# Experts phase: down products one pair late, down weights asked one expert late, rows gathered before the first weights

## The reference, cut to what matters

```
def run_block(args):
    xblk, e = args
    return (jax.nn.silu(xblk @ w_gate[e]) * (xblk @ w_up[e])) @ w_down[e]
```

## Time and profile before

| | |
|---|---|
| median of three runs | 4578.34 us |
| the profiled execution | 4582.33 us |
| its span | 4580.5 us |
| mean granted TensorE clock over the span | 0.912 of full speed |
| PE busy, share of the span | 3719.3 us, 81% |
| experts phase of layer 0, first weights asked to last down product | 1945.1 to 2647.4 us |
| experts phase of layer 1, the same | 3808.1 to 4502.6 us |

### The profile page before, as it was taken

The page is one execution under the profiler, slowest core; times in us unless marked ns, Lnnn a source line. Parts: engine busy times, 40 slices in busy tenths (PEclk is TensorE's granted clock), DMA queues, the critical chain, the costliest instruction groups (busy, mean ns, idle before and its releaser), DMA issues. The chain is left out here.

```text
span 4580.5 us, 88111 instructions
## 1 busy us (share of the span) xinstructions
PE 3719.3 (81%) x34274; PEld 2393.4 (52%) x34275; DVE 1880.4 (41%) x4412; ACT 1370.2 (30%) x3094; POOL 590.2 (13%) x926
## 2 busy tenths in 40 slices
PE   4998995698898866589999817998999766999972
PEld 1786553588888845133333306895666552333321
DVE  3322554677777554300000055415777651000004
ACT  2211564366665322011111112114666411111111
POOL 0000000144444130200000021100000011000001
PEclk6999997899999987699999958999999877999986
DMA  7221001222222154786899962213000414679995
GB/s 291 89 89 70 9 10 41 43 65 80 74 76 75 37 174 174 228 340 262 304 363 388 397 253 102 89 58 145 10 10 10 133 73 198 242 299 387 408 428 210
DMA packets 252931, 771.21 MB, mean 168 GB/s; under 512 B 77908, under 2 KB 166248, under 8 KB 221896
## 3 DMA queue, kind: packets, MB, share of 16 engines
q1 hardware_dynamic: 200488, 639.85, 37.5%
q10 hardware_dynamic: 37584, 78.13, 4.5%
q0 software_dynamic: 14544, 48.79, 2.8%
HBM read 641.22 MB, written 117.60 MB: 166 GB/s over the span
## 5 line engine op out<-in xcount | busy, mean ns | idle before, releaser
L3238 PE MATMUL ex_bY<-ex_w,ex_aT 128*64 x880 | 389.1, 595 | 73.7 <-DVE ex_aT L3301 73.7
L3238 PE MATMUL ex_bG<-ex_w,ex_xT 128*64 x880 | 405.2, 615 | 39.4 <-SPq L3159 26.7
L3241 PE MATMUL ex_bG<-ex_w,ex_xT 128*64 128x512 f32 x880 | 405.3, 615 | 0.0
L3241 PE MATMUL ex_bY<-ex_w,ex_aT 128*64 128x512 f32 x880 | 389.4, 595 | 0.0
L3241 PE MATMUL ex_bU<-ex_w,ex_xT 128*64 128x512 f32 x880 | 386.6, 592 | 0.0
L3238 PE MATMUL ex_bU<-ex_w,ex_xT 128*64 x880 | 386.6, 592 | 0.0
L3299 DVE TENSOR_TENSOR ex_a<-ex_sg,ex_bU 128x512 f32<-128x512 f32 x55 | 37.9, 688 | 813.6 <-PE ex_bU L3241 813.6
L3238 PEld LDWEIGHTS ex_bG<-ex_w,ex_xT 128*64 128x64 f32 x880 | 123.9, 142 | 302.6 <-issue 302.6
L3238 PEld LDWEIGHTS ex_bY<-ex_w,ex_aT 128*64 128x64 f32 x880 | 116.0, 137 | 299.9 <-issue 299.9
L1036 DVE TENSOR_SCALAR_CACHE_REDUCE ad_p<-ad_S 128x512 f32<-128x512 f32 (+1 forms) x384 | 215.6, 600 | 99.8 <-PE ad_S L946 99.7
L3238 PEld LDWEIGHTS ex_bU<-ex_w,ex_xT 128*64 128x64 f32 x880 | 120.6, 137 | 247.4 <-issue 247.4
(11 more groups left out here) (467 smaller groups left out, 8545.5 us busy)
## 6 DMA issues: line engine op xcount, KB each, us to landing
ex_w<-in_moe_w_gate SPq DMA_DIRECT2D x64, 2048.0 KB, 12.2
ex_w<-in_moe_w_up SPq DMA_DIRECT2D x64, 2048.0 KB, 16.4
ex_w<-in_moe_w_down SPq DMA_DIRECT2D x64, 2048.0 KB, 15.0
yb_dram<-ex_y ACTq DMA_DIRECT2D x55, 512.0 KB
rt_mw<-in_mod_w SPq DMA_DIRECT2D x24, 1024.0 KB, 9.4
n_mw<-in_mod_w SPq DMA_DIRECT2D x16, 1024.0 KB, 8.8
kb_dram<-rs_pout SPq DMA_DIRECT2D x60, 256.0 KB, 2.8
rs_KB<-kb_dram SPq DMA_DIRECT2D x120, 128.0 KB, 2.7
```

The lines of the kernel that those rows point to most:

```text
L3238: nc.tensor.matmul(bank[0:BR, :], stationary[:, k, 0:BR], w[:, ds(slot0 + (offset + k * n), 512)], start=k == 0, stop=k == tiles - 1)
L3241: m = nc.tensor.matmul(bank[BR:P, :], stationary[:, k, BR:P], w[:, at:at + 512], start=k == 0, stop=k == tiles - 1)
```

## The change

On PE a pair's down products move behind the next pair's gate and up products and row transposes; its transposes of `a` come after the down products of the pair before. The first pair's gate, up and transposes stand ahead of the loop, the last pair's down products behind it. Each of the three parts of a pair now reads and splits its own code from the table (`where`). The first gate products wait for the first half of the turned rows only, and for the second half at k = 4. On SyncE the down weights of expert o - 1 are asked in the step of expert o, behind its gate and up; each ask reads expert and pair count anew; nothing is asked before GpSimd has issued the first gather (`first_asked`). On GpSimd the gather comes first and the clearing after it. ScalarE and VectorE follow PE's order. The number of matmuls, transposes, copies and bytes is as before.

```diff
@@ -3158,31 +3158,45 @@
-    def step(o, u, free, before):
+    def ask(part, o, u, free):
         e = load(sp, ds(o + T_EXP, 1), NE - 1)
-        tiles = load(sp, ds(o + (T_PEND - WR), 1), NPM, 1) if free else None
-        for part in range(3):
-            fetch(u, e, tiles, part)
-            if before is not None:
-                arrived(*before, part)
-
+        fetch(u, e, load(sp, ds(o + (T_PEND - WR), 1), NPM, 1) if free else None, part)
+
+    def step(o, u, free_gu, free_down, times, seen):
+
+        v = (u - 1) % WR
+        for part in range(2):
+            ask(part, o, u, free_gu)
+            if times is not None:
+                arrived(v, times, part)
+        if times is not None:
+            ask(2, o - 1, v, free_down)
+            if seen is not None:
+                arrived((u - 2) % WR, seen, 2)
+
+    sp.wait_ge(first_asked, 1)
     for o in range(WR):
-        step(o, o, False, (o - 1, 1) if o else None)
+        step(o, o, False, False, 1 if o else None, 1 if o > 1 else None)
...
-    with sp.Fori(1, NE // WR) as i:
+    step(WR, 0, True, False, 1, 1)
+
+    rounds = (NE - WR - 1) // WR
+    with sp.Fori(1, rounds + 1) as i:
         for u in range(WR):
-            step(WR * i + u, u, True, (u - 1, i + 1) if u else (WR - 1, i))
-    left = NE % WR
-    for u in range(left):
-        step(NE - left + u, u, True, (u - 1, NE // WR + 1) if u else (WR - 1, NE // WR))
-    for part in range(3):
+            step(WR * i + 1 + u, (1 + u) % WR, True, True, i + 1, i + 1 if u else i)
+    for o in range(WR * (rounds + 1) + 1, NE):
+        step(o, o % WR, True, True, (o - 1) // WR + 1, (o - 2) // WR + 1)
+    for part in range(2):
         arrived((NE - 1) % WR, (NE - 1) // WR + 1, part)
+    ask(2, NE - 1, (NE - 1) % WR, True)
+    for o in range(NE - 2, NE):
+        arrived(o % WR, o // WR + 1, 2)
...
@@ -3192,11 +3206,12 @@
 def _(pool):
-    nc.gpsimd.memset(zero[:, :], 0.0).then_inc(zeroed, 1)
-    n = load(pool, slice(T_NP, T_NP + 1), NPM)
     nc.gpsimd.tensor_copy(idx[:, :], tok[:, 0:1]).then_inc(idx_done, 1)
     pool.wait_ge(idx_done, 1)
     nc.gpsimd.indirect_dma_start(x[:, :], None, rows[:, :], bass.IndirectOffsetOnAxis(idx[:, 0:1], 0)).then_inc(x_in, 16)
+    pool.sem_inc(first_asked, 1)
+    nc.gpsimd.memset(zero[:, :], 0.0).then_inc(zeroed, 1)
+    n = load(pool, slice(T_NP, T_NP + 1), NPM, 2)
     with pool.Fori(0, n) as i:
...
@@ -3223,46 +3238,66 @@
-    turn(0, False)
-    with pe.Fori(0, n) as i:
-
+    def where(i):
         code = load(pe, ds(i + T_CODE, 1), WR * WR * (NE + 1) - 1, WR * WR)
-        need, slot1 = code // (WR * WR), code % WR
-        slot0 = (code % (WR * WR)) // WR * WCOLS
-
-        def products(bank, stationary, tiles, offset, n, done):
-
-            for u in range(WR):
-                with pe.If(slot1 == u):
-                    for k in range(tiles):
...
-        pe.wait_ge(w_ready[0], need)
-        pe.wait_ge(xT_done, 2 * i + 2)
-        products(bG, xT, KT, 0, EH, g_done)
-        pe.wait_ge(w_ready[1], need)
-        products(bU, xT, KT, UP, EH, u_done)
-        turn(i + 1, True)
-
-        pe.wait_ge(a_done, i + 2)
+        return code // (WR * WR), (code % (WR * WR)) // WR * WCOLS, code % WR
+
+    def products(bank, stationary, at, tiles, offset, n, done, second=None):
+
+        need, slot0, slot1 = at
+        for u in range(WR):
+            with pe.If(slot1 == u):
+                for k in range(tiles):
+                    if second is not None and k == tiles // 2:
+                        pe.wait_ge(xT_done, second)
+                    nc.tensor.matmul(bank[0:BR, :], stationary[:, k, 0:BR], w[:, ds(slot0 + (offset + k * n), 512)],
...
+                    col = u * WCOLS + offset + k * n
...
+                m.then_inc(done, 1)
+
+    def hidden(i, part):
+        at = where(i)
+        pe.wait_ge(w_ready[part], at[0])
+        if part == 0:
+            pe.wait_ge(xT_done, 2 * i + 1)
+            products(bG, xT, at, KT, 0, EH, g_done, 2 * i + 2)
+        else:
+            products(bU, xT, at, KT, UP, EH, u_done)
+
+    def turn_hidden(i):
+
+        pe.wait_ge(a_done, i + 1)
         for k in range(HT):
             t = nc.tensor.transpose(bA[:, k * P:(k + 1) * P], a[:, k:EH:HT], ident[:, :])
         t.then_inc(atr, 1)
+
+    def down(i):
+        at = where(i)
         pe.wait_ge(aT_done, i + 1)
         pe.wait_ge(ye_act, i + 1)
         pe.wait_ge(ye_dve, i + 1)
-        pe.wait_ge(w_ready[2], need)
+        pe.wait_ge(w_ready[2], at[0])
         for b in range(2):
-            products(bY[b], aT, HT, DOWN + b * 512, D, y_done)
+            products(bY[b], aT, at, HT, DOWN + b * 512, D, y_done)
+
+    turn(0, False)
+    hidden(0, 0)
+    hidden(0, 1)
+    turn(1, True)
+    turn_hidden(0)
+    with pe.Fori(1, n) as i:
+        hidden(i, 0)
+        hidden(i, 1)
+        turn(i + 1, True)
+        down(i - 1)
+        turn_hidden(i)
+    down(n - 1)
...
-    turned(0)
-    with act.Fori(0, n) as i:
+    def gated(i):
         act.wait_ge(g_done, i + 1)
-
-        act.wait_ge(a_done, i + 1)
         nc.scalar.activation(sg[:, :], bG[:, :], ACT.Silu).then_inc(sg_done, 1)
-        turned(i + 1)
-        act.wait_ge(y_done, 2 * i + 1)
+    def copied(i, least=None):
+        act.wait_ge(y_done, 2 * i + 1 if least is None else least)
...
+    turned(0)
+    gated(0)
+    turned(1)
+    with act.Fori(1, n) as i:
+
+        act.wait_ge(a_done, i)
+        gated(i)
+        turned(i + 1)
+        copied(i - 1)
+    copied(n - 1, 2 * n)
...
-    dve.sem_inc(a_done, 1)
-    with dve.Fori(0, n) as i:
+    def multiplied(i):
...
+    def turned(i):
...
+    def copied(i):
         dve.wait_ge(y_done, 2 * i + 2)
...
+    multiplied(0)
+    turned(0)
+    with dve.Fori(1, n) as i:
+        multiplied(i)
+        copied(i - 1)
+        turned(i)
+    copied(n - 1)
```

More of the change, by code:

```diff
@@ L3134, in experts_phase @@
             "g_done", "u_done", "sg_done", "a_done", "atr", "aT_done", "y_done", "ye_act", "ye_dve", "y_out"))
-        go, ended, filled, zeroed = (s.sem(n) for n in ("go", "ended", "filled", "zeroed"))
+        go, ended, filled, zeroed, first_asked = (s.sem(n) for n in ("go", "ended", "filled", "zeroed", "first_asked"))
         zero = s.sb("zero", [P, D])
@@ L3212, in _ @@
                 pe.wait_ge(c_in, 16)
-                n = load(pe, slice(T_NP, T_NP + 1), NPM)
+                n = load(pe, slice(T_NP, T_NP + 1), NPM, 2)
                 def turn(i, again):
@@ new lines, in where @@
+                    return code // (WR * WR), (code % (WR * WR)) // WR * WCOLS, code % WR
[7 more added lines that the diff above has]
+                                nc.tensor.matmul(bank[0:BR, :], stationary[:, k, 0:BR], w[:, ds(slot0 + (offset + k * n), 512)],
+                                                 start=k == 0, stop=k == tiles - 1)
+                                col = u * WCOLS + offset + k * n
+                                m = nc.tensor.matmul(bank[BR:P, :], stationary[:, k, BR:P], w[:, col:col + 512], start=k == 0, stop=k == tiles - 1)
+                            m.then_inc(done, 1)
@@ L3292, in _ @@
             def _(dve):
-                n = load(dve, slice(T_NP, T_NP + 1), NPM)
+                n = load(dve, slice(T_NP, T_NP + 1), NPM, 2)
                 dve.sem_inc(ye_dve, 1)
-                dve.sem_inc(a_done, 1)
-                with dve.Fori(0, n) as i:
+                def multiplied(i):
                     dve.wait_ge(sg_done, i + 1)
```

9 lines of the change are left out of this document (2 added, 7 removed).

## The result

| | before | after |
|---|---|---|
| median of the runs | 4578.45 us (4574.96 to 4579.10, 4 runs) | 4608.19 us (4602.55 to 4613.15, 4 runs) |
| the profiled execution, its span | 4582.33, 4580.5 us | 4602.55, 4600.8 us |
| mean granted TensorE clock | 0.912 | 0.906 |

The medians are 29.7 us apart; the ratio of the runs is 1.0058, 95% interval 1.0045 to 1.007, or 27 us. The changed kernel is slower. The prediction said 4571 us, range 4544 to 4594.

The account below looks back on a forecast made before the run. PE was taken to bound each layer's earlier pairs and DMA the last ones. Layer 1's +4.1 and layer 0's -11.9 gave -7.8 us on the median 4578.3, forecast 4571 us, range 4544 to 4594.

Parts of the forecast that it names:

- the start: Start of each layer: gather issued 0.9 us earlier, half the turned rows suffice; -2.0 us in layer 0, -1.7 in layer 1.
- first pair and last pair: Ends of each layer's phase: +6.3 us said for layer 0, -1.1 for layer 1.
- the pairs between, without the circle: Pairs where PE sets the pace: overlap hides the wait before down products; -32.2 us in layer 0, -22.9 in layer 1.
- the circle: Last pairs: loads wait for late down products and PE for loads; 39.2 us per pair against 31.2; +16.0 and +31.9.
- The wait before the last down products of layer 0: Layer 0's end: last down weights asked only when the previous pair's down products end; +7.5 us.
- My link of 14.1 us: In the circle: gate weights asked 1.93 us after the down ask, landing 12.2 us after that, 14.1 together.
- A pair without weight waits: Gate to gate on PE in the first regime: 22.3 us after the change, bounds 22.1 and 22.4.
- The rival that would have put it down to PE's queue: Table read and branches before down products not hidden: 0.5 us a pair, +22, 4593 us; chance 0.18.
- First stretch: First 24 pairs of layer 0 and 20 of layer 1, DMA allowance included: -33.4 and -24 us.
- the prediction's own test: For the whole sum: the forecast falls if either of the two large terms, -57 and +53, is off by a third.
- My allowance for DMA: First stretch: 6.5 us in layer 0 and 5 in layer 1 added for DMA work exceeding PE's time.
- the wait only moves: Wait leaves the down products for another place, pair stays near 23.8 us: +66, 4637 us; chance 0.03.

Follow-up runs that it names:

- tail_old_6: Changed kernel with the last six pairs of each layer in the old order on PE, ScalarE and VectorE; 4559.11 us against 4587.07 before, ratio 0.9939.
- turns_split: Changed kernel with the four transposes of `a` put two and two behind each half of the down products; ratio to before 1.0111.
- pe_one_read: Changed kernel with one table read on PE for gate and up products instead of two; ratio to before 1.0052, pair 22.67 us.
- signal_early: Changed kernel with SyncE waiting for and signalling an expert's gate weights ahead of the down ask; ratio to before 1.0021.
- rows_first: Kernel before, with only the gather issued ahead of the clearing and the first weights asked behind it; 4577.14 us against 4587.07, ratio 0.9978.
- tail_3_and_6_early: Changed kernel with the old order for the last three pairs of layer 0 and six of layer 1, plus early gate signal; 4547.65 us against 4589.41, 0.9904.

## Why the prediction was wrong, point by point

Said and measured, in us against before, each counted from the phase's own first transfer; measured from the two traces:

| step | layer 0, said | measured | layer 1, said | measured |
|---|---|---|---|---|
| the start | -2.0 | -7.1 | -1.7 | -5.0 |
| first pair and last pair | +6.3 | +8.9 | -1.1 | -0.4 |
| the pairs between, without the circle | -32.2 | -13.5 | -22.9 | -8.6 |
| the pair before the circle (layer 1) | | | 0 | +0.9 |
| the circle | +16.0 | +16.7 | +31.9 | +30.0 |
| the pair behind it | | | -2.1 | -1.1 |
| sum | -11.9 | +5.0 | +4.1 | +15.8 |

- **The circle: right**, in place, mechanism and size. 38.7 us on the mean of four pairs against 39.2; DMA's share 0.85 and 0.82 against "about 0.8"; gate products wait 14 to 15 us, as said. The first of the four takes 36.94 us and not 38 to 40: its gate products still run at the full clock, 6.91 us against 8.3 to 9.6. One name was wrong: the ask ahead of the gate of b is that of expert a - 1, not of a. It waits for the same pair, p - 2, so the time is the same. The wait before the last down products of layer 0 is there too: 8.91 us at 2642.71, on the timeline of PE,
```profile
2642.71 1.11 PE L3253 MATMUL ex_bY<-ex_w,ex_aT 128*64 x1 [8.91 <-SPq L3159]
```
 and `tail_old_6` confirms it by taking it away. My link of 14.1 us was right in sum, but not as I read it: with the asks 0.7 us apart it was 13.7.
- **A pair without weight waits: the second step that failed, a term mis-sized**, 22.3 said, 22.67 measured, outside my bounds of 22.1 to 22.4. I took "about 0.1 at each change of kind" once for the pair. The rows above give it: 6.92 + 6.97 + 7.02 for the products instead of 20.7, 1.09 and 0.68 for the transposes instead of 1.1 and 0.5. `turns_split` shows 0.17 us for each further change. Before, the two groups of transposes stood side by side, and a pair had two changes of kind; after, they stand apart, and it has four. Two more at 0.17 make 0.35. Over 24 and 19 pairs it is 0.37 x 43 = 16 us. The rival that would have put it down to PE's queue named nearly the right time, 22.8, for the wrong reason: see `pe_one_read`.
- **First stretch: the step that failed.** I allowed 6.5 and 5 us for DMA (the figures beside them give 5.4 and 4.2), nothing for SyncE and nothing for the clock. Measured were 560.4 - 24 x 22.67 = 16.3 us in layer 0, and 442.9 - 19 x 22.67 = 12.2 in layer 1, 17 more than allowed: 20.5 us are waits for a late signal, 8.0 us the lower clock in the pairs behind them. I had followed the *asks* behind the new wait, but not the *signals*: `arrived` stands in the same queue, so it is late too, wherever three experts come in two pairs. I had the rule in hand, what is queued behind the waiting instruction, and applied it to the last pairs alone. `signal_early` takes all of it away but the wait of pair 24. Of the -55.1 us said for the pairs between, -22.1 came; by the prediction's own test, a large term off by a third, the forecast as a whole falls. My allowance for DMA was not baseless: with the signals in time the loads take back a part behind the stretch.
- **The start: mis-sized the other way.** I let the gather's 11.7 us stand; ahead of the weights it takes 8.1. The two starts together gave -12.1 us instead of -3.7, and `rows_first` alone is 9.9 us faster than before. The half of the turned rows gave the 0.7 said: from turn to gate 2.35 us and not 3.10.
- **Net.** The first stretch lost 33 us (16 + 17) against the forecast, the start gave 8 back, the rest lost 4: 28.6 us between the -7.8 said and the +20.8 of the two phases. More than half of it, 17 us, is one thing: what stands behind a waiting down ask, which I saw in the last pairs and missed in the first stretch. That the forecast did not miss by more is luck, for the start erred the other way. The chance of 0.03 for the rival "the wait only moves" was too small: of the 63 us of idle time that left the down products, 20 came back before gate products of the first stretch, and the clock took 8 more.
- **The bandwidth.** After and `tail_3_and_6_early` have stretches at 405 to 425 GB/s and a share of 1.00; the DMA engines are full there, at a rate well over 358. The 358 GB/s that the Trainium skill gives in "DMA: Bandwidth & Descriptors", section "Where 436 GB/s comes from", is no bound for this kernel. Another page of the Trainium skill, "Perfetto Trace Analysis", section "Roofline", says why: the figure is the share when both cores of a pair draw, and a single core is bound by its DMA engines at about 435 GB/s. By that one, the traces agree: no stretch shown here goes over 425 GB/s.

## What to carry to other kernels

Where a change puts a wait into an in-order queue, list everything that stands behind it in that queue, signals as much as asks, at every place of the loop and not only where the resource is scarce. A row that says "waits for SyncE" does not say that data is late: compare the landing with the product before the wait is priced. A pair that is longer without idle time wants a look at the granted clock and at the pair before it. Work moved behind later work frees its buffers later; where the ring is just deep enough, keep the old order for that stretch, as the last pairs here.

## What the runs showed of the hardware that I had not expected

- A change from products to transposes or back costs the array about 0.17 us with everything ready (23.02 against 22.67 us for two more).
- Two 2 MB loads asked 0.68 or 1.97 us apart, of nearly idle engines, with the store of `y` and more weights asked right behind: the second lands 13.7 or 14.1 us after the first was asked. The distance of the asks hardly counts.
- An indirect gather of 128 rows takes 8.1 us from issue to the first transpose when the weights are asked 0.8 us behind it, 11.7 when they are asked at the same time. Over all runs it is 7.0 to 10.0 us with the gather first, and 11.3 to 11.8 with the weights at the same time or 2.4 us ahead.
- After some 14 us of idle time the array starts at half clock (1.11 us for its first product), and its gate products take 8.3 to 9.6 us from start to start instead of 6.9; so a wait that closes a circle costs more than itself. The granted clock over the circle pairs is 0.81.
- A short wait can do it too. After 2.96 us of idle time the granted clock was 0.50 for 6.83 us, and the pair took 25.52 us and not 22.67; after 2.74 us (at 2337.84) it stayed at 1.00. Without the waits (`signal_early`) it stayed at 1.00 over both first stretches.
